# Routing tables of a top-2-of-32 MoE built in two parts beside the first experts, and a router that reads unscaled rows

## What is computed

```python
h = h + hybrid_mixer(...)                    # ends with y @ w_out
h = h + hier_moe(rmsnorm(h, norm_ffn_g), ...)

def hier_moe(x2d, ...):                      # x2d is the normed h
    g_logits = x2d @ w_rg + b_rg             # 4 groups
    g_sel = argmax(g_logits); p_group = softmax(g_logits)[g_sel]
    e_logits = (x2d @ w_re + b_re)[g_sel]    # the 8 experts of that group
    top_p, top_e = top_k(softmax(e_logits), 2)
    gate = p_group * top_p / sum(top_p)
    # tokens are sorted by expert into blocks of 128 slots
    (silu(xb @ w_gate[e]) * (xb @ w_up[e])) @ w_down[e]    # per block
    # results are scaled with gate and added per token
```

## Time and profile before

| | us |
|---|---|
| median of 3 runs | 1511.28 (1510.02 to 1511.88) |
| the profiled execution, its time | 1510.35 |
| its span, first to last instruction | 1508.5 |
| busy: PE, DVE, ACT, POOL | 1367.9, 1030.4, 664.6, 420.6 |
| mean granted clock of PE, as a share of full speed | 0.957 |

### The profile page before, as it was taken

How to read it: one execution, slowest core, us unless ns; L and a number is a source line. 1 busy time by engine, 2 the same in 40 slices (tenths; PEclk the granted TensorE clock), 3 DMA queues, 4 the chain that set the end, 5 groups by cost and what they waited for, 6 DMA issues and landing times. The chain is left out here.

```text
span 1508.5 us, 21819 instructions
## 1 busy us (share of the span) xinstructions
PE 1367.9 (91%) x7326; PEld 1117.2 (74%) x7327; DVE 1030.4 (68%) x1950; ACT 664.6 (44%) x1179; POOL 420.6 (28%) x476
## 2 busy tenths in 40 slices
PE   5989999999999989999999889999539999999950
PEld 4779888789989758888888778899536777777730
DVE  4448999999960567777888754432547777877727
ACT  4347323322121157777777641221016666666612
POOL 1100335322121043555555114100021333333214
PEclk9999999999999999999999989999759999999985
DMA  5030411123223002103442073221457999999718
GB/s 206 29 141 36 143 57 56 57 78 101 90 83 108 19 1 56 24 1 106 100 100 72 1 229 126 97 89 65 170 223 274 346 366 354 357 370 383 272 54 324
DMA packets 88702, 217.40 MB, mean 144 GB/s; under 512 B 24784, under 2 KB 49904, under 8 KB 76328
## 3 DMA queue, kind: packets, MB, share of 16 engines
q1 hardware_dynamic: 77200, 190.45, 36.3%
q0 software_dynamic: 9216, 16.80, 3.0%
q10 hardware_dynamic: 2200, 9.02, 1.5%
HBM read 193.05 MB, written 44.73 MB: 158 GB/s over the span
## 5 line engine op out<-in xcount | busy, mean ns | idle before, releaser
L421 PE MATMUL ps<-hHi,g_lead 128*128 128x512 f32 (+2 forms) x480 | 184.7, 385 | 8.7 <-DVE g_rest L818 7.5
L315 DVE TENSOR_SCALAR_CACHE_REDUCE mask<-score,cand 128x272 bf16<-128x272 f32 (+6 forms) x224 | 185.5, 892 | 4.6 <-DVE cand L334 4.4
L2219 DVE TENSOR_TENSOR w_rest<-wgu,w_lead 128x1024 fp32r<-128x1024 f32 x128 | 156.0, 1223 | 45.1 <-ACT w_lead L2166 43.9
L422 PE MATMUL ps<-hLo,g_lead 128*128 128x512 f32 (+2 forms) x480 | 183.9, 383 | 0.0
L423 PE MATMUL ps<-hHi,g_rest 128*128 128x512 f32 (+2 forms) x480 | 183.0, 381 | 0.0
L1310 DVE TENSOR_TENSOR pL<-ps,pH 128x512 fp32r<-128x512 f32 (+3 forms) x224 | 124.6, 572 | 51.4 <-ACT pH L1245 48.8
L2166 ACT CAST w_lead<-wgu 128x1024 fp32r<-128x1024 f32 x128 | 134.4, 1055 | 38.0 <-PE ps L2112 38.0
L732 POOL TENSOR_TENSOR g_rest<-g_raw,g_lead 128x2048 fp32r<-128x2048 f32 x12 | 55.6, 4633 | 300.8 <-ACT g_lead L588 300.8
L1245 ACT CAST pH<-ps 128x512 fp32r<-128x512 f32 (+3 forms) x224 | 106.2, 493 | 58.0 <-PE ps L1191 57.8
L2110 PE MATMUL ps<-w_lead,x_lead 128*128 128x512 f32 x256 | 114.2, 446 | 6.0 <-DVE w_rest L2219 6.0
L2132 PE MATMUL ps<-wd,hmT 128*128 128x512 f32 x256 | 115.3, 593 | 1.6 <-DVE hmT L2242 1.0
(11 more groups left out here) (349 smaller groups left out, 3399.1 us busy)
## 6 DMA issues: line engine op xcount, KB each, us to landing
wgu<-in_w_exp_gate SPq DMA_DIRECT2D x32, 1024.0 KB, 7.6
wgu<-in_w_exp_up SPq DMA_DIRECT2D x32, 1024.0 KB, 12.6
wd<-in_w_exp_down SPq DMA_DIRECT2D x32, 1024.0 KB, 12.4
g_raw<-in_w_in SPq DMA_DIRECT2D x16, 1024.0 KB, 5.6
gates_d<-stage SPq DMA_DIRECT2D x32, 256.0 KB, 2.0
gt<-gates_d SPq DMA_DIRECT2D x32, 256.0 KB, 3.1
rel_d<-rel_s ACTq DMA_DIRECT2D x1, 4672.0 KB
KR<-kb_d SPq DMA_DIRECT2D x16, 260.0 KB, 6.3
```

What stands on the lines that cost most here:

```text
L315: return dve.tensor_scalar(mask[:, OFF[i]:OFF[i + 1]], score[:, OFF[i]:OFF[i + 1]], thr, 0.0, op, ALU.add, accum_out=cnt[:, i:i + 1])
L421: pe.matmul(dst, x[0], y[0], start=(k == 0), stop=False)
L422: pe.matmul(dst, x[0], y[1], start=False, stop=False)
L2219: dve.tensor_tensor(w_rest[u][:, :, 2 * part:2 * part + 2, :], wgu[u][:, :, 2 * part:2 * part + 2, :], w_lead[part][:, :, :, :].bitcast(F3 ...
```

## The change

Four things, all from the output projection on.

1. The router reads `h1`, the rows before the norm. The norm's weights are loaded a second time as a column (`gcol`, one small DMA) and multiplied into the router's weights once. The row's `rstd` is put on the logits by DVE, in the instruction that adds the bias. PE's order becomes: first part of projection b, `router(b - 1)`, the other parts, `logits(b - 1)`. `logits` waits for the DVE half of the transposed rows only at its fifth matmul. `x2` is still made for the experts, but nobody on PE waits for it. SP no longer waits for `xn2_d` at the block's end; POOL and DVE do in the next one.
2. The tables' block is gone: tables and experts are one block, in which each engine's program calls a part of the tables and goes on to the experts.
3. The tables are in two parts. The first makes tokens of the 32 own blocks alone (`B` has 32 columns, float32r, `A` in four pieces so that PE can start on a piece; L1868 of after), and POOL gathers from `tok_i` directly. The gates' softmax is left out of the choice: the best experts are taken from the logits, and ACT makes two exponents late. The slot weights come from a second product (`BW`, high and low part), the overflow blocks from a third (`BX`), after expert 0 has begun.
4. The clearing of `xs`, `w_lead` of expert 0, and loads move into the tables' time. The tables now lie in the buffers of experts 2 and 3, so SP loads experts 0 and 1 first, expert 2 when the gather of expert 1 has landed, expert 3 when the third product is done.

```diff
                 def router(b):
-                    pe.wait_ge(s_x2, b + 1)
+                    pe.wait_ge(s_h1, b + 1)
...
-                            mm = pe.transpose(ps[:, 4 + half, P * k:P * (k + 1)], x2[b % 2][:, c:c + P], ident)
+                            mm = pe.transpose(ps[:, 4 + half, P * k:P * (k + 1)], h1[:, b, c:c + P], ident)
...
+                        if n == 0 and b >= 1:
+                            if b == 1:
+                                pe.wait_ge(s_y2, JOBS)
+                            router(b - 1)
                     mm.then_inc(s_op, 1)
-                    if b == 1:
-                        pe.wait_ge(s_y2, JOBS)
                     if b >= 1:
-                        router(b - 1)
-                    if b >= 2:
-                        logits(b - 2)
+                        logits(b - 1)
                 router(NB - 1)
-                logits(NB - 2)
                 logits(NB - 1)
...
-                    dve.tensor_tensor(rl[:, 36 * b:36 * (b + 1)], ps[:, 6 + b % 2, 0:36], rbias[:, :],
-                                      ALU.add).then_inc(s_rl, 1)
+                    dve.wait_ge(s_r2, b + 1)
+                    dve.scalar_tensor_tensor(rl[:, 36 * b:36 * (b + 1)], ps[:, 6 + b % 2, 0:36], rstd[:, b:b + 1],
+                                             rbias[:, :], ALU.mult, ALU.add).then_inc(s_rl, 1)
...
+                dve.wait_ge(s_wr, 48)
+                dve.tensor_tensor(wr[:, :, :], wr[:, :, :], gcol[:, :].unsqueeze(2).to_broadcast([P, KT, 36]),
+                                  ALU.mult).then_inc(s_wg, 1)
...
+    def loads(sp):
+        for u in range(2):
+            load_gate_up(sp, wts, u, u)
+        for u in range(2):
+            load_down(sp, wts, u, u)
+        sp.wait_ge(wts["G"][1], 16)
+        load_gate_up(sp, wts, 2, 2)
+        load_down(sp, wts, 2, 2)
+        sp.wait_ge(s_sl, 3)
+        load_gate_up(sp, wts, 3, 3)
+        load_down(sp, wts, 3, 3)
...
+    def gathers(pool):
+        for k in range(U):
+            pool.memset(xs[k][:, :], 0.0).then_inc(s_xz, 1)
+        pool.wait_ge(s_xz, U)
+        for k in range(2):
+            pool.wait_ge(s_xos[k], 16 * NB // 2)
+        pool.wait_ge(s_tt, 1)
+        for u in range(U):
+            pool.indirect_dma_start(out=xs[u][:, :], out_offset=None, in_=xn2_d,
...
+            tabs["ranks"](pe)
             xpose(pe, 0, 0, 0, True)
             gate_up(pe, 0, 0, 0, True)
             xpose(pe, 1, 0, 1, False)
+            tabs["late_products"](pe)
...
+            tabs["choose"](dve)
+            tabs["weights"](dve)
+            rest(0, 0, 0)
+            rest(0, 0, 1)
             front(0, 0)
-            for part in range(4):
-                rest(0, 0, part)
+            rest(0, 0, 2)
+            rest(0, 0, 3)
+            tabs["slot_weights"](dve)
+            tabs["overflows"](dve)
+            for part in range(3):
+                rest(1, 1, part)
             front(1, 1)
-            for part in range(4):
-                rest(1, 1, part)
+            rest(1, 1, 3)
+            tabs["late_tokens"](dve)
             hidden(0, 0, True)
```

More of the change, by code:

```diff
@@ L1687, in _ @@
                     if b >= 1:
[L1688 to L1692, removed]
+                        logits(b - 1)
+                    if b < NB - 1:
+                        scaled(b)
+                    turn(b)
+                scaled(NB - 1)
                 logits(NB - 1)
@@ L1762, in moe_tables @@
     iota = con[:, K_IOTA:K_IOTA + P]
[L1763 to L1792, removed]
@@ L1793, in moe_tables @@
-    oved = t("r_oved", 32)
-    assert o[0] <= R_H + 33280
-    A = at("r_A", [P, N2, P], F32, wts["end"])
-    ovf, ovf2 = (at(f"r_ovf{k}", [P, 16, NE], F32, wts["end"] + 8192 + 2048 * k) for k in range(2))
+    gm, m3 = (t(EARLY, f"r_g{k}", NB) for k in range(2))
+    eq4 = t(EARLY, "r_eq4", NB, 4)
+    g1 = t(EARLY, "r_g1", NB, 4)
+    picked = t(EARLY, "r_picked", NB, NG, 8)
+    el = t(EARLY, "r_el", NB, 8)
+    ev = t(EARLY, "r_ev", NB, 8)
+    eq8 = t(EARLY, "r_eq8", NB, 8)
+    oh8 = t(EARLY, "r_oh8", 2, NB, 8)
@@ new lines, in moe_tables @@
+    both = t(EARLY, "r_both", NB, NE, dt=BF16)
+    later = t(EARLY, "r_later", N2, 7)
+    B = t(EARLY, "r_B", N2, NE, dt=F32R)
+    OH = t(LATE, "r_OH", 2, NB, NE)
+    prod = t(LATE, "r_prod", 2, NB, NE)
+    eqm = t(LATE, "r_eqm", N2, NE)
+    eqx = t(LATE, "r_eqx", N2, NOV)
+    A = t(LATE, "r_A", N2, P, dt=F32R)
+    BW = t(LATE, "r_BW", N2, 2, NE, dt=F32R)
+    BX = t(LATE, "r_BX", N2, 3, NOV, dt=F32R)
+    e4 = t(SMALL, "r_e4", NB, 4)
+    gs, ws, dif = (t(SMALL, f"r_w{k}", NB) for k in range(3))
@@ new lines, in moe_tables @@
+    top = t(SMALL, "r_top", 2, NB)
+    wgt = t(SMALL, "r_wgt", 2, NB)
+    w_hi = t(SMALL, "r_w_hi", N2, dt=F32R)
+    w_lo = t(SMALL, "r_w_lo", N2, dt=F32R)
+    tot = t(SMALL, "r_tot", NE)
+    over = t(SMALL, "r_over", NE, 7)
+    nov, cumo, ovb, one32 = (t(SMALL, f"r_n{k}", NE) for k in range(4))
+    thr = t(SMALL, "r_thr", 2, 7)
+    e_of, p_of, b_of, q_of, s_of, main_of, extra_of = (t(SMALL, f"r_{n}_of", N2) for n in "epbqsmx")
+    val = t(SMALL, "r_val", N2)
+    owned = t(SMALL, "r_owned", NOV, NE)
@@ L1797, in moe_tables @@
+    tokf, hi, emp, tok2 = (t(SMALL, f"r_tok{k}", NBLK) for k in range(4))
+    oved = t(SMALL, "r_oved", 32)
     keep = R_H
@@ L2000, in moe_tables, with exponents @@
-    return dict(tok_i=tok_i, dst_i=dst_i, slot_w=slot_w, ov_e=ov_e)
+    def loads(sp):
[9 more added lines that the diff above has]
+        load_down(sp, wts, 3, 3)
+    def exponents(act):
+        act.wait_ge(s_rx, 2)
+        act.activation(e4[:, :, :], e4[:, :, :], ACT.Exp).then_inc(s_rx, 1)
+        act.activation(dif[:, :], dif[:, :], ACT.Exp).then_inc(s_rx, 1)
+        act.wait_ge(wts["WG"][0], 32)
+        for part in range(4):
+            act.copy(w_lead[part][:, :, :, :], wts["wgu"][0][:, :, 2 * part:2 * part + 2, :]
+                     ).then_inc(wts["m_wl"], 1)
@@ new lines, in late_products, with link, linked, tt @@
+    def late_products(pe):
+        pe.wait_ge(s_ab, 3 + N2 // PART)
+        for n in range(N2):
+            mm = pe.matmul(ps[:, 7, 0:3 * NOV], A[:, n, :], BX[:, n, :, :].rearrange("p c n -> p (c n)"),
+                           start=(n == 0), stop=(n == N2 - 1))
+        mm.then_inc(s_sl, 1)
+    chain = [0]
+    def link(ins):
+        chain[0] += 1
+        ins.then_inc(s_rt, 1)
+    def linked(dve):
+        dve.wait_ge(s_rt, chain[0])
+    def tt(dve, out, x, y, op):
+        link(dve.tensor_tensor(out, x, y, op))
@@ L2032, in _ @@
         def _(sp):
+            tabs["loads"](sp)
             sp.wait_ge(S["m_gp"], 4)
```

446 lines of the change are left out of this document (230 added, 216 removed).

## The result

The changed kernel takes **1492.01 us** (median; 1491.06 to 1492.97), the kernel before 1510.65 beside it: ratio 0.9876, 95% interval 0.9859 to 0.9894, 18.6 us less. That is 3.6 us above the forecast of 1488.4: inside the range (1484.5 to 1494.0), outside the likeliest case's own (1485.5 to 1490.5). The profiled execution took 1492.95 with a span of 1491.1; before, 1510.35 and 1508.5. The four runs of the changed kernel fall into two pairs, 1491.06 and 1491.08, 1492.95 and 1492.97, and the profiled one is of the upper pair, so its trace is 0.9 us longer than the median.

What follows compares the result with a forecast made beforehand. PE bounds the steady experts and DVE's chain the tables, so an earlier expert start counts in full: 5.4 + 17.8 - 0.8 = 22.4 us off 1510.35 gives 1488.0; stated 1488.4, range 1484.5 to 1494.

Steps and rivals of the forecast that it cites:

- likeliest case: Whole kernel: the main forecast of 1488.4 us, with its own range 1485.5 to 1490.5 and a 79% chance.
- The router's end: Last projection block to the tables: shorter chain after `h1` of block 7, so tables start at 1074.1, 5.4 us earlier.
- the pair ahead: PE, before the last projection's end: one more transposing and logits group, costing 2.6 us and delaying `h1` of block 7.
- the block's change (0.3 idle): Between router and tables: 0.3 us of idle ahead of the tables' `r_g`, taken from the kernel before.
- The tables: Tables' first part on DVE and PE: `tok_i` ready 17.1 us behind the tables' start, where it was 29.2.
- both bounds: PE's narrow float32r table products: a pass costs between 0.03 and 0.196 us; 0.196 was taken, 3.2 us for 16.
- Clearing shut out: Rival, 8%: POOL's clearing gets only DVE's gaps beside the tables, transposes start later; price 6.2 us, total 1494.6.
- The rule which I set against the earlier trace: POOL's clearing beside the tables: two-input DVE instructions shut out only GpSimd instructions reading SBUF, so the 3.6 us clearing passes.
- Gather and transposes: `tok_i` to expert 0's transposes: gather ready at 22.3 us, weights' product decides at 22.6 behind the tables' start, before 40.4.
- Experts 0 and 1: Transposes to expert 1: DVE's queue with 6.8 us of overflow tables starts expert 1 17.6 us behind, 0.8 us lost.
- from here all is as before: From expert 1's start on: unchanged timing if loads come in time; expert 2 begins 28.8 us behind the transposes.
- the rival of a DMA bound: Rival, 2%: DMA becomes the experts' bound, their 10.0 us period grows by over 0.8 us; 1512 or more.

Runs made afterwards that it cites:

- e6: Kernel before with the router's part alone, SP's wait for the scaled rows' stores moved to the head of its next stretch: 1505.55 us.
- e1: Kernel before with the new projection and router alone, old tables, SP's wait for the scaled rows' stores kept at its stretch's end: 1507.91 us.
- e3: Changed kernel with POOL's clearings held back until DVE's first three table instructions are through: 1491.6 us.
- e10: Kernel before with 40 more semaphore increments on SP ahead of the experts' loop, shifting SP's later code: 1511.26 us.
- e4: Changed kernel with 93 filler matmuls on PE among the tables' products and the first two experts: 1489.81 us.
- e5: Changed kernel with the overflow tables' first seven DVE instructions moved into DVE's wait for the gather: 1488.27 us.
- e9: Changed kernel with later clearing, earlier overflow tables and PE fillers reset to fill remaining gaps, including ahead of expert 1: 1484.33 us.
- e8: Changed kernel with later clearing, earlier overflow tables and PE fillers, none behind the overflow product: 1487.51 us.

## Why the prediction came out as it did

The forecast put the profiled execution at 1488.0; it took 1492.95. Step by step, in us:

| step | forecast | measured | difference |
|---|---|---|---|
| `h1` of block 0 starts | 973.34 (as before) | 974.83 | +1.5 |
| blocks 0 to 7 | 92.64 + 2.6 | 95.54 | +0.3 |
| `h1` of block 7 to tables | 5.5 | 5.52 | 0.0 |
| tables to `tok_i` | 17.1 | 17.93 | +0.8 |
| `tok_i` to transposes | 5.5 | 5.85 | +0.35 |
| transposes to expert 1 | 17.6 | 16.96 | -0.6 |
| expert 1 to expert 2 | 11.2 | 12.14 | +0.9 |
| expert 2 to last result | 307.0 | 307.0 | 0.0 |
| last result to end | 53.6 | 55.3 | +1.7 |

**The router's end** was right in each step: the pair ahead costs 2.9 for 2.6, the last logits ran at full clock, and the 5.5 us are the 5.52 of the kernel after and of e6. What I costed at nothing, the move of the stores' wait off the end of the stretch, carries 2.3 of it (e1, e6). I had called that part "the block's change (0.3 idle)", which held only because the wait was moved too. The tables start 3.6 us earlier and not 5.4 because 1.5 was lost ahead of the whole stretch. Of it 0.9 is there at 860 us, ahead of the first instruction that the change touches (one row of each trace, before and after):

```profile
860.32 0.61 POOL L1330 TENSOR_TENSOR otok<-otmp,rec 128x256 f32<-128x256 f32 x1 [5.12 <-DVE otmp L1317]
```
```profile
861.24 0.61 POOL L1330 TENSOR_TENSOR otok<-otmp,rec 128x256 f32<-128x256 f32 x1 [5.12 <-DVE otmp L1317]
```

From that row to `h1` of block 0 the twelve profiled executions took 112.1 to 113.7 us, with the old router as with the new. So a cost of the new router doesn't show there. `h1` of block 0 starts at 973.2 to 973.6 in the four with the old tables and at 973.6 to 975.2 in the eight with the new ones; whether the new code has a part in that stays open. The load of `gcol` held SP for 3.4 us and hid, as forecast.

**The tables** were right as a chain and short by 0.8. The step that failed is the start: two instructions of 0.2 that overlap others took 0.84 and 0.71 (0.57 in `tok_i` by e3). The product's passes cost 0.225 us each and not 0.196, another 0.5 for 16; other small terms gave a little back. A pass thus lies above both bounds that I had set (0.03 and 0.196); the end that I chose was the nearer one, and 32 and 64 columns take the same time at half clock (3.60 and 3.62).

**Clearing shut out** falls: 3.66 us beside the tables, 3.62 alone. The rule which I set against the earlier trace rows holds here (the Trainium skill, SBUF — State Buffer, SBUF: two separate sides): a clearing that reads nothing goes through beside DVE's instructions with two inputs. It was DVE that paid, in a place where I looked for no loss.

**Gather and transposes.** I gave the step from `tok_i` to the issue 0.1 us for the semaphore. It took 1.0, and the kernel before has the same 1.0 between its index copy and its gather, in the brackets of the gather's row: I had read the row and left its bracket out. Issue to transposes then took 4.84, less than the 5.07 that I had summed. The order of the two was also wrong, though by little: the gather decides (idle 0.28 for it), not the weights' product.

**Experts 0 and 1.** Expert 1's start is DVE's queue, as worked out, and 0.6 better. The step that failed is "from here all is as before", with its 11.2 us from expert 1 to expert 2. The gap and the low clock were there before too: PE idled 3.02 us ahead of expert 1, and its matmuls took 0.63 us for 3.1 us behind that, until here (kernel before):

```profile
1139.38 0.61 PE L2110 MATMUL ps<-w_lead,x_lead 128*128 128x512 f32 x1
1139.81 0.41 PE L2111 MATMUL ps<-w_rest,x_lead 128*128 128x512 f32 x1
```

In the kernel after the gap was 2.64 us and the low clock lasted 5.2, so that expert 1 to 2 took 12.1. The change isn't needed for that: with the old tables and the same gap of 3.02 us, e1, e10 and e6 had the low clock for 3.4, 3.7 and 6.1 us and took 11.25, 11.31 and 12.63 from expert 1 to 2. I had taken the 11.2 of one execution as fixed, and it was the shortest of the nine that have the gap. e4, e5 and e9, which close the gap to under 1 us, have 9.74 to 9.77. So the clock behind the wait costs 1.5 to 2.9 us beside the wait itself: e5 gained 2.75 by the wait and 2.4 by the clock. What sets how long the clock stays low isn't shown. The loads were not late anywhere, and the rival of a DMA bound had no support: 347 and 375 GB/s in the steady part with PE busy 20 of 20 us.

**The last stage** had no term in the sum, as nothing of it is changed, and was 1.7 us longer. It is the largest single difference, and its cause is open.

The time fell into the range, but 3.2 of the 5.0 us in the table (the stretch ahead and the last stage) belong to no term or rival of the prediction; without them the sum would have been 1.8 short, inside the forecast's own range. The time is also close to the second rival's 1490 to 1492, and not by that rival's causes: the last logits ran at full clock and `h1` was served at once; only the slow first instructions and the costlier passes, 1.0 us together, are of its kind.

## What to carry to other kernels

When a chain is shortened, list every wait at the boundary behind it: one that was long over (here a store) becomes the last to end, and takes back nearly half the gain (2.3 of 5.1 us). Idle PE ahead of a stretch of matmuls has two prices, the wait and the lower clock of the matmuls behind it; price both, and fill the gap where it can't be closed. Look, too, at what is queued behind each wait of the engine that bounds: seven instructions of 2.7 us in all, moved into a gap of 3.3 us, gave 3.7 us.

## What the runs showed of the hardware

- **A clearing on POOL holds certain DVE instructions.** `r_val` and `r_thr`, each with one input from SBUF and constants, took 0.84 and 0.71 us beside it and both ended at about 1076.84. One of the four clearings takes 3.66/4 = 0.92 us, and the first thus ended at 1076.78. With the clearing started behind them they took 0.22 and 0.16. The reduce and the two-input instructions beside the clearing took 0.19 to 0.61 us, as long as in e3, where they run beside it too. So DVE was held to the end of one instruction of POOL that had started 0.14 us earlier, and POOL not at all. The rows agree with what the Trainium skill says (SBUF — State Buffer, SBUF: two separate sides, its part Who interferes with whom): a scalar operation of DVE can want the port pair that it shares with GpSimd, and whoever issues first keeps the other out for its whole instruction. I had weighed that page's rule on two inputs and not this one.
- **The first indirect DMA starts 1.0 us behind its release.** From the end of the index's instruction to the issue of the first gather: 1.0 us in all twelve profiled executions, whether POOL's own copy or DVE releases it, and in the kernel after 4.8 us more to landing. The later gathers of the kernel before are issued 0.85 to 0.88 us behind their index copy.
- **float32r passes with few columns** took 0.225 us each at a granted clock of 0.50 with 32 and with 64 columns, and 0.123 (1.97/16, 48 columns) to 0.129 (2.06/16, 64 columns) at 1.00.
- **The clock behind a gap.** PE idle of 0.91 us (e5) or 0.32 (e9) ahead of expert 1 left its matmuls at full clock; idle of 2.50 (e8), 2.64 (after) and 3.02 us (before, e1, e10, e6) was followed by 0.63 us matmuls instead of 0.39 for 3.5, 5.2 and 3.1, 3.4, 3.7 and 6.1 us. The length of the slow stretch thus doesn't follow the gap's length alone.
